# Block attention of a prompt: dividing by the row sum on the output tile, with sample pieces two rounds earlier

## The chip, the cores and the metric

The kernel runs on one core of a Trainium2 chip. Its engines are TensorE (PE, matrix products, with PEld for its weight loads), VectorE (DVE), ScalarE (ACT), GpSimd (POOL) and SyncE (SP, which here issues the loads). The metric is the device time of one execution in microseconds (us); less is better. The kernel before takes 1871.77 us, the median of three runs (1870.25 to 1883.65).

## The reference: what is computed

The reference is one inference step of a two-layer decoder trunk, in float32, for a prompt of 512 tokens and for 8 samples of 8 new tokens each, with 1024 cached tokens behind every sample. Layer 0 runs a state space mixer (S5) beside block-sparse attention (8 heads of 64); layer 1 runs HGRN2 beside stick-breaking attention; each layer ends with an output projection, a ConvFFN and a gated embedding. The change touches the attention of layer 0 for the prompt alone. Cut to that:

```
logits = jnp.einsum('bhqd,bhqnkd->bhqnk', q_c, kg) * scale        # scale = 64 ** -0.5
mask = val_c[..., None] & (kpos <= pos_c[None, None, :, None, None])
logits = jnp.where(mask, logits, NEG)
w = jax.nn.softmax(logits.reshape(bsz, nh, qc, nsel * MOBA_BLOCK), axis=-1).reshape(logits.shape)
return jnp.einsum('bhqnk,bhqnkd->bhqd', w, vg)
```

With 512 prompt tokens there are two blocks of 256, so that for the prompt every block in the past is selected, and the result is plain causal attention. For the samples there are four cached blocks of which three are kept, and the new tokens; this part is unchanged and is done in what the text calls the samples' pieces.

## The kernel before, in words

The work of layer 0 before the attention leaves queries and keys in `zqk` (head dimension on the partitions, two heads to a column c) and values in `vt` (tokens on the partitions). The order on every engine is written out by hand; the engines meet through counting semaphores. A fence (all three compute engines wait for each other) stands ahead of the attention stage and behind it.

The stage works through 32 units `UNITS`: head pair c (4), query tile i of 128 tokens (4), and the two heads hh of the pair. A unit has i+1 key tiles, so 128 to 512 keys. Its steps are: PE writes the scores (L1492) into one of two PSUM banks; DVE adds the causal mask on the last 128 columns (L1575), takes the row maximum (L1576) and scales it (L1579); ACT takes the exponential into SBUF and sums each row (L1544); DVE takes the reciprocal of the sum (L1585) and multiplies the probabilities by it (L1586); PE transposes them, 128 columns at a time (L1520), into two other banks; ACT copies them to SBUF (L1554); PE multiplies with the values (L1504), two heads side by side on 64 output rows each, with the values as weights, into bank 4, in which the output of a head pair collects; ACT copies that to `y` once for four query tiles (L1532). Each engine has a loop over rounds u: in round u PE does the scores of u+1, the transpositions of u-1 and, in odd rounds, the outputs of the pair of units u-3 and u-2; DVE does the maximum of u and the normalisation of u-1; ACT the exponential of u and the copy of u-1.

At the end of a round `between` runs pieces of the samples' attention. There are four sample pairs, each a generator on PE, ACT and DVE whose pieces are due at round 8 i + d, with d from the table `DUE_A`. PE's six pieces of a pair are: key products of the first and second sample (L1383 and, behind the second, L1390 for the new tokens' keys), transpositions of the weights (L1397, L1398), value products of the first and second sample (L1408), turn of the output (L1416). DVE's five: scores of the new tokens and block sums (L1617, L1619); block maxima (L1621, L1622); choice of blocks (L1624 to L1631); scaling of the output (L1634, L1635, L1461); copies to `y` (L1468). ACT's three: two pieces of exponentials (L1595, L1599), and the copy of the transposed weights (L1425, L1426). The cached keys and values come by DMA, 256 KB a page of 128 tokens, in an order that SP waits out (`sp_stream`); a buffer is filled again when PE has used it (`k_used`, `v_used`).

For the last pair, DVE's fourth piece begins with `dve_out_first` (L372), the low part of the output projection's first weights and of half of `y`; it waits for ACT's part of the same, `act_out_first` (L369), which ACT does in its round 32. The projection itself is L606, behind the fence.

## Time and profile before

| | us |
|---|---|
| median of three runs | 1871.77 (1870.25 to 1883.65) |
| the profiled execution, its own time | 1887.05 |
| its span, first to last instruction | 1885.3 |
| attention stage of layer 0, in the span | 211.9 to 328.7, 116.8 long |
| PE busy over the span | 1787.7 (95%) |
| DVE busy | 1134.8 (60%) |
| ACT busy | 734.1 (39%) |

Busy time counts instructions of an engine; matrix products overlap each other and their weight loads, so a busy PE is not a PE at its peak. PEclk is the clock that PE was granted, as a share of 2.4 GHz. The chain of waits follows the work that ended last back in time; a piece of it has a start, a length, and the engine and line. f32 products show as two instructions each.

### The profile page before, as it was taken

The page shows a single profiled execution, that of the slowest core. Times are in us where ns is not written, and L with a number is a line of the kernel's source. Part 1 is how long each engine was busy: PE and PEld are TensorE (multiplying, and loading weights), DVE is VectorE, ACT ScalarE, POOL GpSimd, SP SyncE. Part 2 cuts the span into 40 slices and gives each one's busy share as a digit, 9 for nine tenths or more (in the row PEclk, how much of TensorE's full clock was granted, in tenths as well). Part 3 has the DMA queues.
Part 4 walks back from the last instruction along what each step waited for, and adds up shares of the span by engine and source line. Part 5 has one row for each costly group of instructions (what it writes and reads, how often), then busy time and mean ns, then how long its engine had stood idle before and what let it go on. Part 6 is the DMA issues. An engine that isn't in the chain of part 4 may idle for free.

```text
span 1885.3 us, 34376 instructions
## 1 busy us (share of the span) xinstructions
PE 1787.7 (95%) x13464; PEld 1622.6 (86%) x13464; DVE 1134.8 (60%) x2371; ACT 734.1 (39%) x1321; POOL 36.0 (2%) x65
## 2 busy tenths in 40 slices
PE   6899798999999999999999998888999999999997
PEld 5789455999999999989799985445999999999997
DVE  7975356568777762256525855666468777762264
ACT  5222335553333342256323323656553333342253
POOL 1400000000000000000000000000000000000000
PEclk9999788999999999999999996989999999999999
DMA  4124577313222232132121142863313222132111
GB/s 182 66 28 163 204 267 288 112 43 100 79 88 78 64 132 81 47 118 79 51 95 57 57 150 96 313 225 122 111 35 98 81 79 88 54 136 79 71 64 51
DMA packets 77953, 204.18 MB, mean 108 GB/s; under 512 B 12530, under 2 KB 14882, under 8 KB 77314
## 3 DMA queue, kind: packets, MB, share of 16 engines
q1 hardware_dynamic: 75762, 190.36, 29.8%
q0 software_dynamic: 2064, 12.06, 1.7%
q8 instruction: 88, 1.44, 0.3%
q14 instruction: 39, 0.32, 0.1%
HBM read 190.81 MB, written 10.40 MB: 107 GB/s over the span
## 4 chain that ended last, share of the span: by engine, by line
PE 86%; DVE 8%; ACT 2%; issue 2%; DMA 2%; SPq 1%; DVEq 0%; ACTq 0%; POOLq 0%
PE psum L412 29%; PE psum L1946 15%; PE psum L606 13%; PE psum L2346 7%; PE psum L2303 3%; PE psum L420 3%; PE psum L1408 2%; PE psum L1383 2%; PE psum L865 2%; PE psum L2496 1%; PE psum L526 1%; PE psum L540 1%; PE psum L1492 1%; PE psum L1520 1%; PE psum L2559 1%
## 5 line engine op out<-in xcount | busy, mean ns | idle before, releaser
L412 PE MATMUL psum<-sb_a_sb_r,sb_ring_r 128*128 128x288 f32 x1408 | 297.6, 296 | 0.0
L412 PE MATMUL psum<-sb_a_sb_r,sb_arena_r 128*128 128x288 f32 x1344 | 276.5, 296 | 0.0
L412 PE MATMUL psum<-sb_y_sb_r,sb_ring_r 128*128 128x288 f32 x960 | 263.3, 299 | 0.6 <-DVE sb_ring_r L372 0.6
L412 PEld LDWEIGHTS psum<-sb_a_sb_r,sb_ring_r 128*128 128x128 f32 x1408 | 231.3, 188 | 0.3
L372 DVE TENSOR_TENSOR sb_ring_r<-sb_ring,sb_ring_r 128x1024 fp32r<-128x1024 f32 (+1 forms) x90 | 116.2, 1295 | 177.7 <-ACT sb_ring_r L369 176.7
L412 PEld LDWEIGHTS psum<-sb_a_sb_r,sb_arena_r 128*128 128x128 f32 x1344 | 217.0, 188 | 0.0
L412 PE MATMUL psum<-sb_y_sb_r,sb_arena_r 128*128 128x288 f32 x704 | 207.2, 294 | 6.3 <-DVE sb_a_sb_r L372 6.2
L369 ACT ACTIVATE sb_ring_r<-sb_ring 128x1024 fp32r<-128x1024 f32 (+1 forms) x90 | 99.9, 1114 | 289.2 <-PE psum L412 172.3
L412 PEld LDWEIGHTS psum<-sb_y_sb_r,sb_ring_r 128*128 128x128 f32 x960 | 175.5, 190 | 1.5 <-DVE sb_ring_r L372 1.0
L369 ACT ACTIVATE sb_arena_r<-sb_ring 128x1024 fp32r<-128x1024 f32 x90 | 92.9, 1055 | 171.6 <-PE psum L412 149.5
L606 PE MATMUL psum<-sb_arena_r 128*128 128x288 f32 x960 | 156.9, 297 | 1.0 <-DVE sb_arena_r L372 0.9
L1946 PE MATMUL psum<-sb_arena_r,sb_ring_r 128*128 128x288 f32 x1056 | 142.9, 295 | 0.5 <-issue 0.5
L1946 PE MATMUL psum<-sb_arena_r,sb_y_sb_r 128*128 128x288 f32 x1056 | 142.4, 295 | 0.1
L1946 PEld LDWEIGHTS psum<-sb_arena_r,sb_ring_r 128*128 128x128 f32 x1056 | 141.0, 188 | 0.9 <-issue 0.9
L412 PEld LDWEIGHTS psum<-sb_y_sb_r,sb_arena_r 128*128 128x128 f32 x704 | 134.6, 191 | 8.2 <-DVE sb_ring_r L372 6.3
L1946 PEld LDWEIGHTS psum<-sb_arena_r,sb_y_sb_r 128*128 128x128 f32 x1056 | 140.5, 188 | 0.5 <-issue 0.5
L606 PEld LDWEIGHTS psum<-sb_arena_r 128*128 128x128 f32 x960 | 138.6, 188 | 2.4 <-DVE sb_arena_r L372 1.4
L372 DVE TENSOR_TENSOR sb_arena_r<-sb_ring,sb_arena_r 128x1024 fp32r<-128x1024 f32 x74 | 89.3, 1223 | 68.0 <-ACT sb_arena_r L369 67.4
L565 DVE SCALAR_TENSOR_TENSOR sb_a_sb<-sb_a_sb,sb_vec,sb_rstd 128x288 f32<-128x288 f32 x96 | 48.3, 514 | 81.5 <-ACT sb_rstd L513 81.5
L2346 PE MATMUL psum<-sb_a_sb_r,sb_ring_r 128*128 128x288 f32 x448 | 92.0, 297 | 0.0
L372 DVE TENSOR_TENSOR sb_y_sb_r<-sb_ring,sb_y_sb_r 128x1408 fp32r<-128x1408 f32 x16 | 26.0, 1625 | 90.1 <-ACT sb_y_sb_r L369 90.1
L606 PE MATMUL psum<-sb_y_sb_r,sb_arena_r 128*128 128x288 f32 x256 | 75.2, 294 | 0.0
(406 smaller groups left out, 3176.3 us busy)
## 6 DMA issues: line engine op xcount, KB each, us to landing
sb_ring<-w SPq DMA_DIRECT2D x166, 512.0 KB, 3.5
sb_ring<-wd SPq DMA_DIRECT2D x32, 704.0 KB, 4.2
sb_arena<-sb_v SPq DMA_DIRECT2D x64, 256.0 KB, 5.3
sb_arena<-moba_v SPq DMA_DIRECT2D x56, 256.0 KB, 5.3
sb_ring<-moba_k SPq DMA_DIRECT2D x32, 256.0 KB, 5.6
sb_a_sb<-moba_k SPq DMA_DIRECT2D x32, 256.0 KB, 7.5
sb_ring<-sb_k SPq DMA_DIRECT2D x32, 256.0 KB, 6.0
sb_a_sb<-sb_k SPq DMA_DIRECT2D x32, 256.0 KB, 6.5
```

The costliest lines, as they stand in the source:

```text
L369: e.eng.activation(fr(dst), src, ACT.Copy).then_inc(ready, 1)
L372: e.eng.tensor_tensor(fr(dst), src, fr(high).bitcast(F32), ALU.subtract).then_inc(ready, 1)
L412: ins = e.eng.matmul(out[:, half, :], fr(w[p][:, k, :]), fr(x[q][:, k, cols]), start=(first and k == 0 and i == 0), stop=(last and k == kb ...
L420: ins = e.eng.matmul(out[:, half, :], w[:, k, :], rhs[:, k, half * HALF:(half + 1) * HALF], start=(first and k == 0), stop=(last and k == ...
L565: e.eng.scalar_tensor_tensor(a[:, k, c], a[:, k, c], vcol(layer, gain, k), rstd[:, c], ALU.mult, ALU.mult)\
L606: ins = e.eng.matmul(out, fr(w[p][:, k, :]), fr(x[q][:, k, COLS[half]]), start=(k == 0 and i == 0), stop=(k == KD - 1 and i == 2))
L865: last = e.eng.matmul(psum[0:n, 2 * t.s, :], fr(x[:, k, i * P:i * P + n]), fr(w[:, :, k, :]), start=(k == 0 and j == 0), stop=(k == KD - 1 ...
L1383: last = pe.matmul(psum[32 * c:32 * c + 32, 5 + half, :], qz[:, c, i, s, :], keys[:, 4 * half:4 * half + 4, c, :], start=(s == 0), stop=(s ...
L1408: last = pe.matmul(s_out[32 * c:32 * c + 32, s * P:(s + 1) * P], wt[0:rows, g, 32 * c:32 * c + 32], v[0:rows, c * P:(c + 1) * P], start=(g ...
L1946: last = e.eng.matmul(pair(t.s)[:, half, :], fr(dsplit[part][i // 2][:, k, :]), fr(x[:, COLS[half]]), start=(j == 0 and i == 0), stop=(j = ...
L2303: last = e.eng.matmul(psum[0:n, 2 * t.s, :], fr(x[:, k, i * P:i * P + n]), fr(w[:, :, k, :]), start=(k == 0 and z == 0), stop=(k == KD - 1 ...
L2346: last = e.eng.matmul(pair(t.s)[:, half, :], fr(pair_c(m)[p][:, k, :]), fr((a, y)[q][:, k, COLS[half]]), start=(k == 0 and i == 0), stop=( ...
```

## The change

The probabilities are no longer multiplied by the reciprocal row sum. They go to the transposition as the exponential left them, and the division is done on the unit pair's output. For that the output products swap their operands: the transposed probabilities (128 keys x 128 queries) are the weights and 64 value columns are streamed, so the output of two heads stands as 128 queries x 128 columns in bank 3 or 4; DVE takes two reciprocals at once (L1596) and multiplies each head's 64 columns from PSUM into SBUF (L1600), PE turns the tile (L1520 of the new kernel) and ACT copies it to `y` (L1543), once a pair instead of once in four. The transposed probabilities are written back into the unit's own score bank, and three banks take turns. A unit's transpositions now stand ahead of the scores of the unit two later. Row maxima, sums and reciprocals have rings of 4 and 8 columns. The samples' pieces are due two rounds earlier on PE, ACT and DVE, and the loops end at round 37 instead of 33 or 32.

```diff
--- before.py
+++ after.py
@@ -1302,7 +1302,7 @@
             for x in range(u, 8 * NPAIR + 16) if u == last else [u]:
                 for i, p in enumerate(pieces):
                     for d in units:
-                        if apart * i + d == x:
+                        if max(apart * i + d, 0) == x:
                             next(p, None)
 
         kv_in = [sem(f"kv_in{i}") for i in range(4)]
@@ -1472,13 +1472,18 @@
 
         pb = [cut(unit_at + i * 512, 512) for i in range(2)]
         ptb = [cut(unit_at + (2 + i) * 512, 512).rearrange("p (j n) -> p j n", j=4) for i in range(4)]
-        stat = small[:, 8:64]
-
-        sco_ready, nmx_ready, prob_ready, pn_ready, ptr_ready, pt_ready, o_unit, o_copied = (
-            sem(x) for x in ("sco_ready", "nmx_ready", "prob_ready", "pn_ready", "ptr_ready", "pt_ready", "o_unit", "o_copied"))
-        UNITS = [(2 * c + hh, i) for c in range(4) for i in range(4) for hh in range(2)]
-
-        DUE_A = {"pe": (8, (1, 2, 6, 7, 8, 9)), "act": (8, (5, 5, 6)), "dve": (8, (3, 4, 5, 9, 9))}
+        onb = [cut(unit_at + 6 * 512 + i * P, P) for i in range(2)]
+        assert unit_at + 6 * 512 + 2 * P <= 27952
+        most, nmost, total, share = (small[:, 8 + 8 * i:16 + 8 * i] for i in range(4))
+
+        sco_ready, nmx_ready, prob_ready, ptr_ready, pt_ready, o_unit, o_normed, o_turned, o_copied = (
+            sem(x) for x in ("sco_ready", "nmx_ready", "prob_ready", "ptr_ready", "pt_ready", "o_unit", "o_normed",
+                             "o_turned", "o_copied"))
+        PAIRS = [(c, i) for c in range(4) for i in range(4)]
+        UNITS = [(2 * c + hh, i) for c, i in PAIRS for hh in range(2)]
+
+        DUE_A = {"pe": (8, (-1, 0, 4, 5, 6, 7)), "act": (8, (3, 3, 4)), "dve": (8, (1, 2, 3, 7, 7))}
+        LAST_A = len(UNITS) + 5
 
         def pe_moba_prompt(e):
             pe = e.eng
@@ -1487,78 +1492,84 @@
             def scores(u):
                 hh, i = UNITS[u]
                 r0, c, n = 64 * (hh % 2), hh // 2, P * (i + 1)
-                if u >= 2:
-                    pe.wait_ge(prob_ready, u - 1)
-                pe.matmul(psum[:, u % 2, 0:n], zqk[r0:r0 + 64, c, i * P:(i + 1) * P], zqk[r0:r0 + 64, 4 + c, 0:n],
+                if u >= 3:
+                    pe.wait_ge(pt_ready, u - 2)
+                pe.matmul(psum[:, u % 3, 0:n], zqk[r0:r0 + 64, c, i * P:(i + 1) * P], zqk[r0:r0 + 64, 4 + c, 0:n],
                           start=True, stop=True).then_inc(sco_ready, 1)
 
-            def outputs(u):
-                c, i = UNITS[u][0] // 2, UNITS[u][1]
-                pe.wait_ge(pt_ready, u + 2)
-                if i == 0 and c >= 1:
-                    pe.wait_ge(o_copied, c)
-                for j in range(i + 1):
-                    for x in (u, u + 1):
-                        hh = UNITS[x][0]
-                        r0 = 64 * (hh % 2)
-                        last = pe.matmul(psum[r0:r0 + 64, 4, i * P:(i + 1) * P],
-                                         vt[:, j, hh * HD:(hh + 1) * HD], ptb[x % 4][:, j, :],
-                                         start=(j == 0), stop=(j == i))
-                        if j == i:
-                            last.then_inc(o_unit, 1)
+            def turned(u):
+                pe.wait_ge(prob_ready, u + 1)
+                for j in range(UNITS[u][1] + 1):
+                    last = pe.transpose(psum[:, u % 3, j * P:(j + 1) * P], pb[u % 2][:, j * P:(j + 1) * P], ident)
+                last.then_inc(ptr_ready, 1)
+
+            def outputs(p):
+                c, i = PAIRS[p]
+                pe.wait_ge(pt_ready, 2 * p + 2)
+                if p >= 2:
+                    pe.wait_ge(o_copied, p - 1)
+                for hh in range(2):
+                    at = (2 * c + hh) * HD
+                    for j in range(i + 1):
+                        last = pe.matmul(psum[:, 3 + p % 2, HD * hh:HD * hh + HD], ptb[(2 * p + hh) % 4][:, j, :],
+                                         vt[:, j, at:at + HD], start=(j == 0), stop=(j == i))
+                    last.then_inc(o_unit, 1)
+
+            def output_turned(p):
+                pe.wait_ge(o_normed, p + 1)
+                pe.transpose(psum[:, 3 + p % 2, P:2 * P], onb[p % 2], ident).then_inc(o_turned, 1)
 
             scores(0)
-            for u in range(len(UNITS) + 2):
-                if u + 1 < len(UNITS):
-                    scores(u + 1)
+            scores(1)
+            for u in range(LAST_A + 1):
                 if 1 <= u <= len(UNITS):
-                    hh, i = UNITS[u - 1]
-                    pe.wait_ge(pn_ready, u)
-                    if u >= 3:
-                        pe.wait_ge(pt_ready, u - 2)
-                    for j in range(i + 1):
-                        last = pe.transpose(psum[:, 2 + (u - 1) % 2, j * P:(j + 1) * P],
-                                            pb[(u - 1) % 2][:, j * P:(j + 1) * P], ident)
-                    last.then_inc(ptr_ready, 1)
-                if u >= 3 and u % 2 == 1:
-                    outputs(u - 3)
-                between(samples, u, len(UNITS) + 1, DUE_A["pe"])
+                    turned(u - 1)
+                    if u + 1 < len(UNITS):
+                        scores(u + 1)
+                if u % 2 == 1:
+                    p = u // 2
+                    if 1 <= p <= len(PAIRS):
+                        outputs(p - 1)
+                    if 2 <= p <= len(PAIRS) + 1:
+                        output_turned(p - 2)
+                between(samples, u, LAST_A, DUE_A["pe"])
 
         def act_moba_prompt(e):
             act = e.eng
 
-            def copy_out(c):
-                act.wait_ge(o_unit, 8 * (c + 1))
-                act.activation(y[:, 4 + c, 0:TP], psum[:, 4, :], ACT.Copy).then_inc(o_copied, 1)
+            def copy_out(p):
+                c, i = PAIRS[p]
+                act.wait_ge(o_turned, p + 1)
+                act.activation(y[:, 4 + c, i * P:(i + 1) * P], psum[:, 3 + p % 2, P:2 * P], ACT.Copy).then_inc(o_copied, 1)
 
             act.wait_ge(stored, 16 * 5)
             act.preload_act_table_set("natural_log_exp_and_others")
             samples = [act_moba_sample(e, i) for i in range(NPAIR)]
-            for u in range(len(UNITS) + 1):
+            for u in range(LAST_A + 1):
                 if u < len(UNITS):
-                    hh, i = UNITS[u]
-                    n = P * (i + 1)
+                    n = P * (UNITS[u][1] + 1)
                     act.wait_ge(nmx_ready, u + 1)
                     if u >= 2:
                         act.wait_ge(ptr_ready, u - 1)
-                    act.activation(pb[u % 2][:, 0:n], psum[:, u % 2, 0:n], ACT.Exp, scale=ATT_SCALE,
-                                   bias=stat[:, 2 + u % 2:3 + u % 2], accum_out=stat[:, 4 + u % 2:5 + u % 2])\
+                    if u >= 8:
+                        act.wait_ge(o_normed, (u - 8) // 2 + 1)
+                    act.activation(pb[u % 2][:, 0:n], psum[:, u % 3, 0:n], ACT.Exp, scale=ATT_SCALE,
+                                   bias=nmost[:, u % 4:u % 4 + 1], accum_out=total[:, u % 8:u % 8 + 1])\
                        .then_inc(prob_ready, 1)
                 if u == len(UNITS):
                     act_out_first(e, 0, sco_ready)
-                if u >= 1:
-                    hh, i = UNITS[u - 1]
+                if 1 <= u <= len(UNITS):
+                    i = UNITS[u - 1][1]
                     act.wait_ge(ptr_ready, u)
                     if u >= 5:
                         act.wait_ge(o_unit, u - 4)
-                    act.activation(ptb[(u - 1) % 4][:, 0:i + 1, :], psum[:, 2 + (u - 1) % 2, 0:P * (i + 1)]
+                    act.activation(ptb[(u - 1) % 4][:, 0:i + 1, :], psum[:, (u - 1) % 3, 0:P * (i + 1)]
                                    .rearrange("p (j n) -> p j n", j=i + 1), ACT.Copy).then_inc(pt_ready, 1)
-                if u >= 10 and (u - 10) % 8 == 0:
-                    copy_out((u - 10) // 8)
+                if u >= 6 and u % 2 == 0:
+                    copy_out((u - 6) // 2)
                 if u == len(UNITS):
                     act_slab(e, out_pairs[1], 1)
-                    copy_out(3)
-                between(samples, u, len(UNITS), DUE_A["act"])
+                between(samples, u, LAST_A, DUE_A["act"])
 
         def dve_moba_prompt(e):
             v, do = e.eng, e.st.do
@@ -1566,26 +1577,30 @@
             dve_queries(e)
             samples = [dve_moba_sample(e, i) for i in range(NPAIR)]
             causal = lcon[:, LCON[0]["causal"]:LCON[0]["causal"] + P]
-            for u in range(len(UNITS) + 1):
+            for u in range(LAST_A + 1):
                 if u < len(UNITS):
-                    hh, i = UNITS[u]
+                    i = UNITS[u][1]
                     n = P * (i + 1)
                     v.wait_ge(sco_ready, u + 1)
-                    own = psum[:, u % 2, i * P:n]
+                    own = psum[:, u % 3, i * P:n]
                     do(v.tensor_tensor(own, own, causal, ALU.add))
-                    do(v.tensor_reduce(stat[:, u % 2:u % 2 + 1], psum[:, u % 2, 0:n], AXX, ALU.max))
-                    if u >= 2:
-                        v.wait_ge(prob_ready, u - 1)
-                    v.tensor_scalar(stat[:, 2 + u % 2:3 + u % 2], stat[:, u % 2:u % 2 + 1], -ATT_SCALE, None, ALU.mult)\
+                    do(v.tensor_reduce(most[:, u % 4:u % 4 + 1], psum[:, u % 3, 0:n], AXX, ALU.max))
+                    if u >= 4:
+                        v.wait_ge(prob_ready, u - 3)
+                    v.tensor_scalar(nmost[:, u % 4:u % 4 + 1], most[:, u % 4:u % 4 + 1], -ATT_SCALE, None, ALU.mult)\
                      .then_inc(nmx_ready, 1)
-                if u >= 1:
-                    w = u - 1
-                    n = P * (UNITS[w][1] + 1)
-                    v.wait_ge(prob_ready, w + 1)
-                    do(v.reciprocal(stat[:, 6 + w % 2:7 + w % 2], stat[:, 4 + w % 2:5 + w % 2]))
-                    v.tensor_scalar(pb[w % 2][:, 0:n], pb[w % 2][:, 0:n], stat[:, 6 + w % 2:7 + w % 2], None, ALU.mult)\
-                     .then_inc(pn_ready, 1)
-                between(samples, u, len(UNITS), DUE_A["dve"])
+                if u >= 4 and u % 2 == 0 and (u - 4) // 2 < len(PAIRS):
+                    p = (u - 4) // 2
+                    at = 2 * p % 8
+                    v.wait_ge(o_unit, 2 * p + 2)
+                    do(v.reciprocal(share[:, at:at + 2], total[:, at:at + 2]))
+                    if p >= 2:
+                        v.wait_ge(o_turned, p - 1)
+                    for hh in range(2):
+                        last = v.tensor_scalar(onb[p % 2][:, HD * hh:HD * hh + HD], psum[:, 3 + p % 2, HD * hh:HD * hh + HD],
+                                               share[:, at + hh:at + hh + 1], None, ALU.mult)
+                    last.then_inc(o_normed, 1)
+                between(samples, u, LAST_A, DUE_A["dve"])
 
 
         def act_moba_sample(e, i):
```

PE's order over rounds 2 to 7 of the first pair in the kernel before (L1492 scores, L1520 transpositions, L1504 outputs, L1397 and L1398 the samples' weights; repeats of a unit's rows are left out at the ends):

```order
L1492 MATMUL psum<-sb_arena 128x512
L1520 MATMUL psum<-sb_con,sb_arena 128x128 x3
L1504 MATMUL psum<-sb_arena 64x128 x4
L1492 MATMUL psum<-sb_arena 128x512
L1520 MATMUL psum<-sb_con,sb_arena 128x128 x3
L1397 MATMUL psum<-sb_con,sb_arena 128x128 x8
L1398 MATMUL psum<-sb_con,sb_arena 64x128
L1492 MATMUL psum<-sb_arena 128x128
```

The same place in the changed kernel (L1497 scores, L1503 transpositions, L1514 outputs, L1520 turn of an output):

```order
L1503 MATMUL psum<-sb_con,sb_arena 128x128 x2
L1497 MATMUL psum<-sb_arena 128x384
L1397 MATMUL psum<-sb_con,sb_arena 128x128 x8
L1398 MATMUL psum<-sb_con,sb_arena 64x128
L1503 MATMUL psum<-sb_con,sb_arena 128x128 x3
L1497 MATMUL psum<-sb_arena 128x512
L1514 MATMUL psum<-sb_arena 128x64 x4
L1520 MATMUL psum<-sb_con,sb_arena 128x128
```

Both score products of 512 keys stood ahead of the samples' weight transpositions, and now stand behind them; a product of 384 keys is the last in front.

DVE's order at the end of the stage before, from the last normalisations (L1585, L1586) through the last pair's fourth and fifth pieces:

```order
L1585 RECIPROCAL sb_small<-sb_small 128x1
L1586 TENSOR_SCALAR sb_arena<-sb_arena,sb_small 128x512
L1634 TENSOR_REDUCE sb_arena<-sb_arena 128x1
L1635 RECIPROCAL sb_arena<-sb_arena 128x1
L372 TENSOR_TENSOR sb_ring_r<-sb_ring,sb_ring_r 128x1024
L372 TENSOR_TENSOR sb_y_sb_r<-sb_y_sb,sb_arena_r 128x288 x4
L1461 TENSOR_SCALAR sb_arena<-psum,sb_arena 128x256
L1468 COPY sb_y_sb<-psum 64x4x8 x4
```

And now (L1590 is the scale of the last unit's maximum, L1596 and L1600 the division of a pair's output):

```order
L1590 TENSOR_SCALAR sb_small<-sb_small 128x1
L1649 TENSOR_REDUCE sb_arena<-sb_arena 128x1
L1650 RECIPROCAL sb_arena<-sb_arena 128x1
L372 TENSOR_TENSOR sb_ring_r<-sb_ring,sb_ring_r 128x1024
L372 TENSOR_TENSOR sb_y_sb_r<-sb_y_sb,sb_arena_r 128x288 x4
L1461 TENSOR_SCALAR sb_arena<-psum,sb_arena 128x256
L1468 COPY sb_y_sb<-psum 64x4x8 x4
L1596 RECIPROCAL sb_small<-sb_small 128x2
L1600 TENSOR_SCALAR sb_arena<-psum,sb_small 128x64 x2
L1596 RECIPROCAL sb_small<-sb_small 128x2
```

The division of the last two pairs' outputs stands behind the split and the samples' last pieces, where nothing of the prompt stood before.

## Rows read from the trace of the kernel before

**Rows 1.** The page, first part: busy us, share, instructions.
```profile
PE 1787.7 (95%) x13464; PEld 1622.6 (86%) x13464; DVE 1134.8 (60%) x2371; ACT 734.1 (39%) x1321; POOL 36.0 (2%) x65
```
**Rows 2.** Windows: stretch, length, busy us of PE, PEld, DVE, ACT, POOL, clock, DMA.
```profile
211.90:328.70 116.80, 105.23 (x1116) 59.48 (x1117) 71.70 (x248) 51.87 (x156) 0.00 (x0) 0.81 0.73 260
254.00:255.00 1.00, 0.30 (x1) 0.00 (x0) 0.93 (x5) 0.42 (x1) 0.00 (x0) 1.00 1.03 381
256.00:265.00 9.00, 8.57 (x28) 4.45 (x28) 6.43 (x25) 4.81 (x18) 0.00 (x0) 0.50 1.05 389
265.00:266.00 1.00, 1.00 (x6) 0.65 (x6) 0.41 (x2) 1.00 (x3) 0.00 (x0) 0.77 0.76 281
```
**Rows 3.** Chain of waits through the stage: start us, us, engine and line.
```profile
223.76 0.27 PE psum L1390 x16
...
251.66 0.27 PE psum L1390 x16
...
256.43 0.31 DVE psum L1575
...
258.09 0.90 PE psum L1520 x3
...
262.88 1.71 PE psum L1397 x8
...
266.92 2.24 PE psum L1408 x72
...
277.41 1.85 PE psum L1383 x16
...
306.65 0.27 PE psum L1390 x16
```
**Rows 4.** Chain of waits, single steps at the full clock: scores, transpositions, outputs; last L2496.
```profile
241.55 0.42 PE psum L1492 x2
241.97 0.59 PE psum L1520 x4
...
244.79 0.63 PE psum L1492 x2
245.42 0.26 PE psum L1520
...
273.28 1.02 PE psum L1504 x16
...
1037.66 3.52 PE psum L2496 x32
```
**Rows 5.** Groups of instructions by shape, DVE, 205 to 345 us: busy us, mean ns | idle.
```profile
L1576 DVE TENSOR_REDUCE sb_small<-psum 128x1 f32<-128x256 f32 x8 | 3.4, 424 | 0.3
L1585 DVE RECIPROCAL sb_small<-sb_small 128x1 f32<-128x1 f32 x32 | 4.9, 154 | 3.9 <-ACT sb_arena L1544 3.9
L1586 DVE TENSOR_SCALAR sb_arena<-sb_arena,sb_small 128x512 f32<-128x512 f32 x8 | 3.9, 487 | 0.3
L1586 DVE TENSOR_SCALAR sb_arena<-sb_arena,sb_small 128x128 f32<-128x128 f32 x8 | 2.3, 288 | 0.3
L1617 DVE SCALAR_TENSOR_TENSOR sb_arena<-psum,sb_lcon 128x64 f32<-128x64 f32 x4 | 0.9, 225 | 3.8 <-PE psum L1390 3.8
```
**Rows 6.** Timeline: start us, us; DVE's piece three begins, ACT's last exponential of the sample ends.
```profile
257.95 0.15 DVE L1624 TENSOR_REDUCE sb_arena<-sb_arena 128x1 f32<-128x4 f32 x1
261.69 0.21 ACT L1599 ACTIVATION_READ_ACCUMULATOR sb_arena<-sb_arena 128x1 f32 x1
```
**Rows 7.** Timeline at the start of the stage: DVE's copies of the samples' queries.
```profile
213.23 0.99 DVE L1436 COPY sb_arena<-sb_arena 64x128 f32<-64x128 f32 x4
```
**Rows 8.** Timeline at the end of the stage: the split ahead of the output projection.
```profile
321.92 1.06 ACT L369 ACTIVATE sb_ring_r<-sb_ring 128x1024 fp32r<-128x1024 f32 x1
323.08 1.22 DVE L372 TENSOR_TENSOR sb_ring_r<-sb_ring,sb_ring_r 128x1024 fp32r<-128x1024 f32 x1 [0.55 <-ACT sb_ring_r L369]
324.23 1.56 DVE L372 TENSOR_TENSOR sb_y_sb_r<-sb_y_sb,sb_arena_r 128x288 fp32r<-128x288 f32 x4
```

## The prediction

> **What bounds the kernel now.** I read the busy slices of the page first, then the windows of the block-attention stage, then its chain of waits, and last the timeline of single rounds. The page [rows 1] shows TensorE (PE) busy for 95% of the span, so that a stage with less is worth a look. The stage of the change, from 211.9 to 328.7 us [rows 2], is one: 116.8 us, 6% of the span, PE busy 105.2 with a mean granted clock of 0.81, VectorE (DVE) 71.7. Nothing outside it is edited, so all that follows is a sum over these 116.8 us.
>
> Within it the samples' pieces come four times, every 8 rounds. The piece that ends a pair's key products, L1390, starts at 223.76 for the first, 251.66 for the second and 306.65 for the fourth [rows 3]: a period of 27.6 us. Take the one that begins at 251.93, where that piece ends. Up to 258.09 the chain runs through DVE; from there to the next L1390 it stays on PE [rows 3]. In the DVE part PE runs out of work (busy 0.30 us between 254 and 255), and its clock falls from 1.00, which is 2.4 GHz, to 0.50, 1.2 GHz, through 256 to 265; in 265 to 266 it is back on 1.00 for about half (0.77) [rows 2], some 7 us after PE's work began again at 258.09 [rows 3]. So there are three costs in a period: PE's own work, a stretch that DVE sets, and low clock behind it.
>
> **PE's work in a round, then and now.** At the full clock the chain gives 0.42 us for a score product of 128 keys and 0.63 for 256, so 0.21 more for each 128: 0.84 and 1.05 for 384 and 512. One transposition costs 0.26, four 0.59, so 0.11 more for each [rows 4]. These pieces keep their cost; only where they stand changes. The output products change form. Before, sixteen L1504 instructions (64-column weights) take 1.02 us, 64 ns each [rows 4]. After, the probabilities are the 128x128 weights and 64 value columns stream. The nearest row is L2496, f32, 128x128 weights and 64 columns: 32 in 3.52 us, **110 ns each** [rows 4]. The stage has 160 of them (80 products, two instructions each), so 17.6 us against 10.2, plus 16 new transpositions of the output at 0.26 or less (the chain's single one), 4.2 us at most. I take 110 ns because that row has the same weights, type and columns; the lower bound is the old 64 ns.
> The Trainium skill (TensorE: Matmul & The Clock Gate, LDWEIGHTS) puts a weight load at columns / 1.2, an estimate of 107 ns for 128 columns, and L2496 agrees. The same page's table in Back-to-back issue gap has about 60 cycles for up to 64 moving columns, 25 ns; by it the 160 would cost 4 us, a saving of 6 us instead of a loss of 7. The trace decides for the first.
>
> Rounds u mod 8 of the new order, at the full clock (transpositions of u-1, scores of u+1, outputs, output turn, sample piece): round 1 is .26+.63+1.76+.26 = 2.9; round 2 .9; round 3 1.9; round 4 .37+.84 = 1.2 and then the samples' nine weight transpositions, 1.14; round 5 .48+1.05+.88+.26 and V0 2.24 = 4.9; round 6 .48+1.05+2.24 = 3.8; round 7 .59+.42+1.32+.26+.37+1.85 = 4.8; round 0 .59+.42+2.12 = 3.1. V is a sample's value products, 2.24, and a sample's key products are 1.85, with 0.27 for L1390 after the second [rows 3]; .37 is the two turns of the sample's output. The sum is **24.7**, against 21.9 for the old pieces by the same rows.
>
> **DVE's share.** Removed are 32 reciprocals at 154 ns and 32 normalisations, 288 ns (128 columns) to 487 ns (512) [rows 5]: 4.9 + 12.4 = 17.3 us. Added are 16 times a reciprocal and two 128x64 operations from PSUM; the nearest row is L1617, 225 ns [rows 5], so 0.55 with its waits, 8.8 us. DVE does 8.5 us less. The score part of a round is the mask (the chain's 0.31), the maximum (0.42 for 256 keys), a small scale like the reciprocal's 0.15, and gaps: 0.95 for 256 keys, and 0.13 more for 384 [rows 3, 5].
>
> **What the two rounds do.** DVE's first three sample pieces move from rounds 3, 4, 5 to 1, 2, 3, ScalarE's (ACT) exponentials to round 3, PE's nine transpositions from 6 to 4. The way from the end of L1390 to these: DVE's pieces one and two lay between 251.93 and 256.43 together with one score part of 384 keys (1.08), a reciprocal of which 0.08 shows and a normalisation of 256 columns (0.35), so they take 4.50-1.51 = 2.99 [rows 3]. In the new rounds 1 to 3 two score parts of 256 keys (.95 each) and one output share (.55) lie among them. Piece three and ACT's exponentials run from 257.95 to 261.90, 3.95 [rows 6], and .1 goes for issue: 2.99+.95+.55+.95+3.95+.1 = **9.5**. PE has only 2.9+.9+1.9+1.2 = 6.9 us to do there, so it waits 2.6. Before, the chain reaches L1397 at 262.88, 10.9 after the same point, but both products of 512 keys had run by then; now they stand behind. Behind the wait stand 1.14+4.9+3.8+4.8+3.1 = 17.8 us of PE. So 9.5+17.8 = 27.3 with the clock never low.
> The gap before the transpositions will cost clock as the old one did. If it returns 7 us after the restart, those 7 us hold the nine transpositions, 1.92 instead of 1.14 (L1397's eight took 1.71 at the low clock), three at .90 for .48 (the chain's at 258.09), and the 512-key scores and the outputs at double, 2.0 and 1.76 for 1.05 and .88 [rows 3, 4]: 3.1 us and with the output's turn 3.2. The bounds are 0 and 3.2; I take 2.5, nearer to the end that before shows. Period: **29.8**, against 27.6.
>
> **Start.** Both key pieces now stand before the first transposition and need the queries, ready at 214.22 [rows 7]. At the low clock the first takes twice 1.85, 3.7; the second ends with L1390 at 220.0 to 222.0, as the clock comes back. I take 221.0; before 224.0 [rows 3]. Gain 3.0 (2 to 4). The key and value transfers run at 381 to 389 GB/s through 254 to 265 and fall to 281 in 265 to 266 [rows 2]; the keys are used after the value products that start at 266.92 and the next ones [rows 3], so they land with a few us to spare. The moves keep their distances and the period grows, so I cost the transfers at nothing; if they were late, that would add. SP's own queue keeps its order. POOL does nothing here.
>
> **End.** After the last L1390 (before: 306.92) two more rounds are left than before. PE ends the last value piece at 9.5+1.1+4.9+3.8+2.5 = 21.8, its next transposition at 22.4. DVE's last sample piece, now in round 31, begins with the split for the output projection, and that waits for ACT: a copy (about .6), the slab 1.06; then DVE 1.22 and 1.56, and a scale near L1586's .49 [rows 5, 8] = 27.4. Before, these ran beside PE's last value products. Now PE's turn of the sample output waits for them, and behind it the last unit: .37+.59, copy .6, outputs 1.76, share .55, turn .26, copy .3, fence .25, with gaps 32.4. Before it is 328.7-306.9 = 21.8 [rows 2, 3].
>
> **Sum.** 221.0 + (29.8-.55, no share in the first) + 2x29.8 + 32.4 = 342.2, against 328.7: +13.5. The wait of about 3.4 us in the last round may leave the clock low for the last outputs and the projection's start: 0 to 5.7 us (2.2 in the tail, 3.5 in 7 us of projection); I take 2. **+15.5 us, 0.8%.** The sum is against the profiled execution, 1887.05 us, which lies 15 us above the median; its span's stage is the only one I have, so I put the difference on the median: 1871.8+15.5 = **1887.3**. The low ends together (clock always full, 220.0) give 331.3, +2.6; the high ends (222.0, 3.2 a period, 5.7 at the end) give +23.
>
> **Rivals.** A measurement of this kernel tells about 1%, 18.7 us, from no change.
> *Same way, clock low longer*: over 1% slower, +18.7 to +23, if the clock returns late in each period and the projection starts low. For it: the low stretch of 256 to 265 outlasted the restart by 7 us, and idle time now comes later and longer; against: both stretches must bite, in every period. 0.24.
> *The clock stays full*: +2.6 to +8. For it: PE now works through rounds 1 to 3, with no gap before round 4. Against: PE's 0.7 idle us in 254 to 255 were followed by the fall [rows 2]. 0.12.
> *PE-paced, faster than before*: one mechanism, in rounds 3 and 4: the sample softmax on DVE and ACT is ready by 6.9 instead of 9.5 after L1390, because the share and the maxima fit in DVE's holes. Then nothing waits: 9.1 + 3x24.7 + a tail of 23.5 (16.7 of rounds and 6.8 for the last units) = 106.7, 10 us less: 1861.7. It decides at 2.6 us off a chain whose every row is measured; 0.09. Beyond that no mechanism reaches 1% (98 us for the stage is below PE's 4x24.7): 0.02.
> *The change moves nothing that matters* (no time on the path differs): 0.03. The forecast itself, +8 to +18.7: 0.50.
> So faster 0.02, same 0.50+0.12+0.09+0.03 = 0.74, slower 0.24. The range 1868 to 1896 takes the forecast, the full clock and the late clock up to +24, and leaves out the PE-paced case and the far ends, under 0.2.
>
> **What the profile after would show.** Right: L1514 at about 110 ns each; L1390 starts near 220.7 and then 29 to 30.5 apart; PE idle 2 us or more before L1397, released by ACT's exponentials; idle before the last L1416, released by DVE's L1461; stage over 125 us. Wrong: L1514 near 64 ns or less, a period at or under 27, no idle at L1397, or a fence before 329.

## The result, and the profile after

The changed kernel takes a median of 1904.0 us (1898.23 to 1907.05, 4 runs) against 1872.74 us (1870.25 to 1883.65, 4 runs) for the kernel before. The ratio of the two kernels over all their runs is **1.0146, interval 1.012 to 1.0173** (the two medians by themselves would give 1.0167): 22 to 32 us slower. The forecast was 1887.3 us with a range up to 1896, so the direction of the sum was right and its size too small by about 12 us of the 27. The profiled execution takes 1907.05 us, its span is 1905.3 us.

The page after, first part (busy us, share of the span, instructions); it answers to [rows 1]:

```profile
PE 1802.1 (95%) x13480; PEld 1640.4 (86%) x13480; DVE 1128.6 (59%) x2355; ACT 735.1 (39%) x1333; POOL 38.4 (2%) x65
```

DVE has 16 instructions less, as the diff says, and 6.2 us less, where the prediction had 8.5; PE has 16 more, and 14.4 us more. The same 95% share hides both. Windows of the stage after, with the columns of [rows 2]: first the whole stage, from the first score product to the first product of the output projection (L606), then stretches with a low clock:

```profile
208.25:346.57 138.32, 119.63 (x1133) 76.76 (x1133) 65.74 (x232) 52.45 (x167) 0.00 (x0) 0.78 0.62 219
257.00:268.00 11.00, 11.00 (x96) 7.93 (x96) 1.79 (x6) 3.58 (x11) 0.00 (x0) 0.50 0.24 87
289.00:292.00 3.00, 2.54 (x12) 2.39 (x12) 0.62 (x2) 1.73 (x8) 0.00 (x0) 0.50 0.86 315
317.00:329.00 12.00, 10.91 (x95) 7.95 (x95) 3.01 (x11) 4.93 (x17) 0.00 (x0) 0.50 0.40 149
337.00:346.00 9.00, 5.79 (x24) 4.92 (x24) 3.69 (x15) 1.99 (x4) 0.00 (x0) 0.50 0.19 59
```

The stage takes 138.3 us instead of 116.8 and its mean clock is 0.78 instead of 0.81. From 257 to 268 PE is busy for every one of 11 us and the clock is still 0.50: this is not waiting, it is the same work at half the speed. Windows of 1 us (stretch, length, PE busy, clock, DMA) date the changes of the clock, estimated from a window's mean clock; two of them:

```profile
254.00:255.00 1.00, 0.75 (x2) 0.89 1.04 381
268.00:269.00 1.00, 1.00 (x4) 0.79 0.13 20
```

By such windows the clock falls at 220.6, 254.8, 288.9 and 316.2 and is back at 234.3, 268.4, 292.3 and 329.9; it falls once more at 336.7 and comes back in the projection. Each fall comes before PE's restart at L1397 (225.16, 256.74, 289.45, 318.08), the first one 4.5 us before it, while PE works: PE had stood idle for 1.50 us before 219.34. So idle time in the rounds ahead of L1397 stands before a fall too, and not only the wait in front of it.

The chain of waits through the stage after (start us, us, engine and line) says which work that is:

```profile
215.85 0.28 PE psum L1390 x16
...
246.70 0.22 PE psum L1390 x16
...
247.81 1.94 PE psum L1514 x16
...
256.74 1.97 PE psum L1397 x8
...
259.56 2.00 PE psum L1497 x2
261.56 1.90 PE psum L1514 x8
...
263.67 4.15 PE psum L1408 x72
...
279.42 0.22 PE psum L1390 x16
...
289.45 1.97 PE psum L1397 x8
...
293.37 1.03 PE psum L1514 x8
...
294.52 2.24 PE psum L1408 x72
...
308.05 0.22 PE psum L1390 x16
...
318.08 1.97 PE psum L1397 x8
...
325.02 4.15 PE psum L1408 x72
...
338.71 0.69 PE psum L1416 x2
...
341.20 3.65 PE psum L1514 x16
...
346.57 33.59 PE psum L606 x240
```

L1390 still marks the end of a pair's key products. Its starts are 30.85, 32.72 and 28.63 apart, against 27.6 in [rows 3] (three periods, called the first, second and third). Behind L1397 in the second period, the 512-key scores (L1497) take 2.00, eight output products (L1514) 1.90 and the value products (L1408) 4.15; at the full clock, in the third period or in [rows 3], the last two take 1.03 and 2.24. The timeline after shows the two waits that the prediction asked for (the first with two rows, weight load and product):

```profile
256.73 0.50 PEld L1397 LDWEIGHTS psum<-sb_con,sb_arena 128*128 128x128 f32 x3 [2.60 <-ACT sb_arena L1614]
256.74 0.69 PE L1397 MATMUL psum<-sb_con,sb_arena 128*128 128x128 f32 x2 [1.98 <-ACT sb_arena L1614]
...
338.71 0.69 PE L1416 MATMUL psum<-sb_con,sb_arena 128*128 128x128 f32 x2 [3.43 <-DVE sb_arena L1461]
```

And the new operations by shape, 205 to 350 us (busy us, mean ns | idle before them); the L1600 and L1596 rows answer to L1586 and L1585 of [rows 5]:

```profile
L1514 PE MATMUL psum<-sb_arena 128*128 128x64 f32 x160 | 25.8, 319 | 0.9 <-ACT sb_y_sb L1543 0.9
...
L1600 DVE TENSOR_SCALAR sb_arena<-psum,sb_small 128x64 f32<-128x64 f32 x32 | 7.6, 280 | 0.6
L1520 PE MATMUL psum<-sb_con,sb_arena 128*128 128x128 f32 x16 | 5.2, 327 | 0.6 <-DVE sb_arena L1600 0.6
...
L1596 DVE RECIPROCAL sb_small<-sb_small 128x2 f32<-128x2 f32 x16 | 2.6, 160 | 7.0 <-PE psum L1514 7.0
```

A mean of 319 ns for L1514 counts products that overlap one another. What each adds to the chain at the full clock is 121 ns (1.94 us for 16 instructions), and 129 ns where there are only eight (1.03 us).

### The profile page after: what moved, and what is told of

Same layout as the page of the kernel before. It is cut to its first block, busy times and chain, and to the rows that moved or that the text cites. A ratio compares the mean times of both kernels' runs of the same rounds, so it can differ in the third digit from the quotient of the medians.

```text
span 1905.3 us, 34397 instructions
## 1 busy us (share of the span) xinstructions
PE 1802.1 (95%) x13480; PEld 1640.4 (86%) x13480; DVE 1128.6 (59%) x2355; ACT 735.1 (39%) x1333; POOL 38.4 (2%) x65
## 4 chain that ended last, share of the span: by engine, by line
PE 85%; DVE 8%; ACT 3%; issue 2%; DMA 2%; SPq 1%; DVEq 0%; ACTq 0%; POOLq 0%
PE psum L412 28%; PE psum L1961 15%; PE psum L606 13%; PE psum L2361 7%; PE psum L2318 3%; PE psum L420 2%; PE psum L1408 2%; PE psum L1383 2%; PE psum L865 1%; PE psum L2511 1%; PE psum L526 1%; PE psum L1514 1%; PE psum L540 1%; PE psum L1497 1%; PE psum L2574 1%
## 5 line engine op out<-in xcount | busy, mean ns | idle before, releaser
L606 PE MATMUL psum<-sb_arena_r 128*128 128x288 f32 x960 | 156.9, 297 | 1.0 <-DVE sb_arena_r L372 0.9
L606 PEld LDWEIGHTS psum<-sb_arena_r 128*128 128x128 f32 x960 | 138.6, 188 | 2.4 <-DVE sb_arena_r L372 1.4
L606 PE MATMUL psum<-sb_y_sb_r,sb_arena_r 128*128 128x288 f32 x256 | 75.2, 294 | 0.0
```

What stands on the lines that cost most here:

```text
L606: ins = e.eng.matmul(out, fr(w[p][:, k, :]), fr(x[q][:, k, COLS[half]]), start=(k == 0 and i == 0), stop=(k == KD - 1 and i == 2))
```

## The experiments

**Theory 1**: the pieces moved two rounds ahead open PE's gap before the samples' weight transpositions (L1397), and the clock that falls in it stays low over the work behind. **The rival**, Theory 2 in the expectations: the new arithmetic (products with the probabilities as weights, division and turn of the output) is what costs, whatever the order. What each says in numbers stands with each run.

A stage has three parts: from its first scores to the end of the first L1390, three periods, and the rest to the first L606. From the chain of each run's one profiled execution, us:

| kernel | start | three periods | end | stage | ratio to before [interval] |
|---|---|---|---|---|---|
| before | 12.1 | 82.9 | 21.8 | 116.8 | 1 |
| predicted | 9.1 | 88.9 | 32.4 | 130.3 | |
| after | 7.9 | 92.1 | 38.3 | 138.3 | 1.0146 [1.012, 1.0173] |
| e8, after again | 8.1 | 94.6 | 37.2 | 139.9 | 1.0144 [1.0128, 1.0159] |
| e1, after, old order | 12.2 | 87.8 | 22.4 | 122.4 | 1.0032 [1.0014, 1.005] |
| e2, before, new order | 8.1 | 91.5 | 35.4 | 135.0 | 1.0122 [1.0086, 1.0159] |
| e9, before, one round | 9.1 | 84.1 | 27.2 | 120.3 | 1.0033 [1.002, 1.0046] |
| e3, after, old products | 8.5 | 81.8 | 31.5 | 121.8 | 1.0088 [1.0058, 1.0117] |
| e6, after, split later | 8.0 | 94.6 | 32.5 | 135.2 | 1.0106 [1.0081, 1.0132] |
| e4, after, 2 dead products | 8.5 | 88.1 | 32.9 | 129.6 | 1.0126 [1.0097, 1.0155] |
| e10, after, 3 dead products | 8.0 | 82.5 | 32.8 | 123.3 | 1.0057 [1.0036, 1.0079] |
| e12, e1 with e4's | 11.3 | 80.8 | 22.7 | 114.7 | 1.0019 [1.0002, 1.0035] |

**e1_due_back.** The changed kernel with the old table of rounds.

```diff
-        DUE_A = {"pe": (8, (-1, 0, 4, 5, 6, 7)), "act": (8, (3, 3, 4)), "dve": (8, (1, 2, 3, 7, 7))}
+        DUE_A = {"pe": (8, (1, 2, 6, 7, 8, 9)), "act": (8, (5, 5, 6)), "dve": (8, (3, 4, 5, 9, 9))}
```

> The changed kernel with the samples' pieces due where they were before (table with 1, 2, 6, 7, 8, 9 for PE, 5, 5, 6 for ACT, 3, 4, 5, 9, 9 for DVE); the division on the output, the score banks and the loops' ends stay as changed. Theory 1 (the two rounds cost most: the samples' softmax has too little PE work in front of it, both 512-key products run behind it at the low clock, and the last split has no cover): a period near 28.3 us, no wait before the last L1416, the stage 120 to 125 us against 138.3, so 14 to 18 us less than the changed kernel, 1878 to 1886. Theory 2 (the swapped output products at 110 ns, and not the rounds, cost most): hardly under the changed kernel, 1895 or more, ratio to before at least 1.011.

1883.72 us against 1876.88, ratio 1.0032. Its stage, with the columns of [rows 2]:

```profile
210.58:332.99 122.41, 107.71 (x1133) 68.87 (x1133) 65.58 (x232) 51.75 (x167) 0.00 (x0) 0.89 0.70 248
```

It issues the same instructions as the changed kernel (x1133 on PE) and PE is busy for 12 us less. Most of the loss goes with the order; the new arithmetic alone costs 3 to 9 us.

**e2_due_only.** The kernel before, with the new table alone.

```diff
-                        if apart * i + d == x:
+                        if max(apart * i + d, 0) == x:
...
-        DUE_A = {"pe": (8, (1, 2, 6, 7, 8, 9)), "act": (8, (5, 5, 6)), "dve": (8, (3, 4, 5, 9, 9))}
+        DUE_A = {"pe": (8, (-1, 0, 4, 5, 6, 7)), "act": (8, (3, 3, 4)), "dve": (8, (1, 2, 3, 7, 7))}
```

> The kernel before with only the new due table (samples' pieces two rounds earlier on all engines), nothing else of the change. Theory 1: most of the loss is here too: the period grows by 2 to 4 us and the tail has the wait for the split, 8 to 18 us above before, 1881 to 1891. Theory 2: within 4 us of before, or faster by the 3 to 4 us that the start gains.

1901.54 us against 1876.88, ratio 1.0122. Its stage:

```profile
208.10:343.08 134.98, 115.39 (x1116) 64.67 (x1117) 71.58 (x248) 52.15 (x155) 0.00 (x0) 0.75 0.63 225
```

The old arithmetic in the new order already has the loss: 18.2 us on the stage, at a clock of 0.75. With e1's 5.6 us the two halves make 23.8, where the two traces of the whole change show 21.5 and 23.1; they add up to within the 1.6 us by which the two traces differ.

**e9_one_round.** The kernel before, its pieces one round ahead instead of two.

```diff
-        DUE_A = {"pe": (8, (1, 2, 6, 7, 8, 9)), "act": (8, (5, 5, 6)), "dve": (8, (3, 4, 5, 9, 9))}
+        DUE_A = {"pe": (8, (0, 1, 5, 6, 7, 8)), "act": (8, (4, 4, 5)), "dve": (8, (2, 3, 4, 8, 8))}
```

> The kernel before with the samples' pieces one round earlier instead of two, nothing else. Two rounds cost 23 us (ratio 1.0122). If the cause is what stands in front of the samples' weight transpositions and of the last split (one 512-key product of the two is back in front, one value piece is back beside the split), one round costs between a third and two thirds of that, ratio 1.004 to 1.008. If the loss comes only with the second round (the start or the ring of buffers), the ratio is under 1.003.

1880.56 us against 1874.65, ratio 1.0033, just under what was expected. One round costs about a quarter of what two cost in e2. The periods hardly grow (84.1 for 82.9), and in its chain L1397 stands right behind PE's own transpositions and outputs (L1504) with no wait between, so it is the second round that opens the wait at L1397; the end grows by 5.4 us a round at first and by 8.2 with the second.

**e3_old_form.** The changed kernel with the value columns as weights again.

```diff
-                for hh in range(2):
-                    at = (2 * c + hh) * HD
-                    for j in range(i + 1):
-                        last = pe.matmul(psum[:, 3 + p % 2, HD * hh:HD * hh + HD], ptb[(2 * p + hh) % 4][:, j, :],
-                                         vt[:, j, at:at + HD], start=(j == 0), stop=(j == i))
-                    last.then_inc(o_unit, 1)
+                for j in range(i + 1):
+                    for hh in range(2):
+                        at = (2 * c + hh) * HD
+                        last = pe.matmul(psum[HD * hh:HD * hh + HD, 3 + p % 2, 0:P], vt[:, j, at:at + HD],
+                                         ptb[(2 * p + hh) % 4][:, j, :], start=(j == 0), stop=(j == i))
+                        if j == i:
+                            last.then_inc(o_unit, 1)
```

> The changed kernel with its output products in the old form (64 value columns as weights, the 128 probabilities streamed, two heads side by side), written to the same banks; everything behind them runs as changed, so the division and the turn work on a tile that stands the wrong way, and the output of the prompt's attention is not the reference's. Theory 1: L1514 back to about 64 ns at the full clock, 7.4 us less at full clock and up to 12 with what ran at the low one: 1892 to 1898. Theory 2: most of the 27 us goes, 1885 or less.

1893.99 us against 1876.88, ratio 1.0088, about 10 us under the changed kernel and inside what Theory 1 gave. The form itself is worth 7.4 us in the sum (160 times 110 less 64 ns). In its profiled execution the clock was back 2.7 to 2.9 us after every L1397, so its stage shows a larger gain (121.8 for 138.3) than the 10 us of the timed runs.

**e5_no_norm.** The kernel before without reciprocal and normalisation.

```diff
-                    pe.wait_ge(pn_ready, u)
+                    pe.wait_ge(prob_ready, u)
...
-                    v.wait_ge(prob_ready, w + 1)
-                    do(v.reciprocal(stat[:, 6 + w % 2:7 + w % 2], stat[:, 4 + w % 2:5 + w % 2]))
-                    v.tensor_scalar(pb[w % 2][:, 0:n], pb[w % 2][:, 0:n], stat[:, 6 + w % 2:7 + w % 2], None, ALU.mult)\
-                     .then_inc(pn_ready, 1)
```

> The kernel before without the division by the row sum (L1585 and L1586 left out, PE's transpositions wait for the exponential instead; the prompt's attention output is then not divided, so not the reference's). It is what the change takes from DVE, 17 us of work, with nothing added in its place and no rounds moved. If DVE's division is what holds the period: 0.4 to 1 us less in each of the rounds 3 to 6, 1.5 to 3 us a period, 6 to 12 us less than before in all. If PE's own work and the clock hold it: within 4 us of before.

1877.3 us against 1875.05, ratio 1.0006 [0.9992, 1.0021]: the second of the two cases, within 4 us of before. Its trace has 64 DVE instructions and 15.2 us of DVE's busy time less in the stage (17.3 by [rows 5]). The whole relief that the change aims at is worth nothing that can be told, even when nothing is added for it: at most 1.5 us by the interval.

**e6_split_later.** The changed kernel; DVE's split for the output projection moves from before its last sample piece to round 33.

```diff
-            if i == NPAIR - 1:
+            if i == NPAIR - 1 and n >= NPAIR:
                 dve_out_first(e)
...
+                if u == len(UNITS) + 1:
+                    dve_out_first(e)
                 between(samples, u, LAST_A, DUE_A["dve"])
```

> The changed kernel with DVE's split for the output projection (L372, 2.8 us) taken out of the last pair's fourth piece and done in round 33, behind the division of the last pair but one, so that the samples' output and the last unit no longer wait for it. If the wait for the split is part of the loss: the wait of 3.4 us before the last L1416 goes and some of the low clock of the tail with it, 4 to 8 us less than the changed kernel. If the last unit's own chain sets the end: 0 to 3 us.

1895.83 us against 1875.05, ratio 1.0106, some 7 us under the changed kernel, though the intervals just overlap. Its periods are those of e8, its end is 32.5 instead of 37.2 us. So the split in front of the last L1416 is about 5 us of the end in these two traces.

**e8_after_again.** The changed kernel unedited, to see what differs between two executions.

> The changed kernel again, unedited, on the same chip and beside the same runs of before as the other three: a ratio of 1.012 to 1.017, and a second trace, which shows how far stages without an edit differ between two runs (HGRN took 43 to 54 us in the traces so far).

1902.11 us against 1875.05, ratio 1.0144. Its chain:

```profile
217.77 0.28 PE psum L1390 x16
...
248.71 0.22 PE psum L1390 x16
...
279.92 0.22 PE psum L1390 x16
...
312.45 0.22 PE psum L1390 x16
...
349.88 2.26 PE psum L606 x8
```

Here the third period is the long one (32.53), in the first trace it was the second (32.72) and the third was short (28.63). One order of instructions, one kernel: how long the clock stays low is not fixed by them. It is back 9.3, 8.4, 11.3 and 9.5 us after PE's restart at L1397 (by windows of 1 us).

**e4_fill.** The changed kernel with two dead products of 512 columns, into a bank whose contents have been used, just ahead of PE's wait for the sample's softmax.

```diff
+            if layer == 0:
+                for _ in range(2):
+                    pe.matmul(psum[:, 7, :], ident, con[:, 0:512], start=True, stop=True)
             pe.wait_ge(sw_ready, n + 1)
```

> The changed kernel with two dead f32 products (identity as weights, 512 columns, 1.7 us at the full clock, into the bank of the samples' new scores, whose contents have been used) ahead of PE's wait for the samples' softmax, four times in the stage. If the low clock behind that wait is the larger part of what the sum missed, the clock stays at 1.00 or comes back earlier, V0 (L1408) takes 2.24 everywhere and the time falls by 6 to 14 us. If the low clock begins earlier than the filler or the filler only delays the work behind it, the time stays or rises by up to 6 us.

1900.09 us against 1876.88, ratio 1.0126. Its interval overlaps that of the changed kernel: inconclusive. In its trace the dead products themselves ran at the low clock in three of four places, wholly or in part, so the clock had fallen before them, in the rounds ahead where PE also waits for DVE and ACT.

**e10_fill3.** As e4, and a third dead product at the start of round 4.

```diff
+            if layer == 0:
+                for _ in range(2):
+                    pe.matmul(psum[:, 7, :], ident, con[:, 0:512], start=True, stop=True)
...
+                if u % 8 == 4 and u < len(UNITS):
+                    pe.matmul(psum[:, 7, :], ident, con[:, 0:512], start=True, stop=True)
```

> The changed kernel with three dead products of 512 columns in round 4 of every eight (one ahead of the round's transpositions, two ahead of the samples' weight transpositions, 2.6 us at the full clock), one more than before, to cover nearly all of PE's 3 idle us there. If the clock falls because of that idle time, it stays at 1.00 up to the transpositions in most periods, L1397 takes about 1.1 instead of 1.97, periods are 28 to 29 us and the ratio 1.008 to 1.011. If low clock is not what lengthens the periods, the ratio stays at 1.0145 or rises by 0.001 to 0.003, as the dead products delay the work.

1884.99 us against 1874.65, **ratio 1.0057**, its interval clear of the changed kernel's: some 16 us are gained by adding work. Its chain, then a window over nearly three periods:

```profile
245.67 0.22 PE psum L1390 x16
...
255.71 1.09 PE psum L1400 x8
...
272.97 0.22 PE psum L1390 x16
...
300.27 0.22 PE psum L1390 x16
```

```profile
246.00:322.00 76.00, 75.46 (x809) 46.56 (x808) 42.43 (x151) 34.89 (x115) 0.00 (x0) 1.00 0.80 289
```

The clock is 1.00 from 246 to 322, the sample's transpositions (L1400 here) take 1.09 instead of 1.97, and the period is 27.3 us: the number that the prediction's sum had for a clock that is never low. The way to the transpositions is no shorter (245.89 to 255.71, 9.8 us); DVE and ACT still set most of it. PE filled its wait and got its clock. What is left of the loss in this trace is the end, 11.0 us, less 4.1 at the start, and 2.3 us in the projection (34.3 for 32.0). The dead products do not reach the last wait, the one for the split; there the clock is low again, and L1514 x16 (L1517 here) takes 3.65 us as in the changed kernel:

```profile
324.00:338.00 14.00, 10.56 (x43) 9.63 (x44) 7.52 (x21) 6.91 (x16) 0.55 (x1) 0.54 0.24 69
```

**e7_before_fill.** The kernel before with one dead product of 512 columns in rounds 4 and 5 of 8, where its own gap lies.

```diff
-                    pe.wait_ge(pn_ready, u)
                     if u >= 3:
                         pe.wait_ge(pt_ready, u - 2)
+                    if u % 8 in (4, 5):
+                        pe.matmul(psum[:, 2 + (u - 1) % 2, :], ident, con[:, 0:512], start=True, stop=True)
+                    pe.wait_ge(pn_ready, u)
```

> The kernel before with one dead f32 product of 512 columns (0.85 us at the full clock, into the transposition bank that the next transpositions overwrite) in rounds 4 and 5 of every eight, ahead of PE's wait for the division. If low clock behind DVE's stretch costs the 3.6 us a period that its rows suggest: the clock stays at 1.00 in most periods and the time falls by 4 to 12 us. If the fall is set by more than these two gaps: no change, or up to 4 us slower.

1873.17 us against 1875.05, ratio 0.9993 [0.9974, 1.0011]: expected was a gain of 4 to 12 us, and none is proven. The profiled stage takes 111.3 us at a clock of 0.94:

```profile
213.20:324.50 111.30, 100.62 (x1132) 54.91 (x1133) 71.70 (x248) 51.55 (x156) 0.00 (x0) 0.94 0.77 273
```

That is 5.5 us less than the one trace of the kernel before, and the timed runs don't follow it. A single trace of this stage is good to some microseconds only.

**e11_fill_start.** As e7, with two more dead products in round 0.

```diff
+                if u == 0:
+                    for _ in range(2):
+                        pe.matmul(psum[:, 2, :], ident, con[:, 0:512], start=True, stop=True)
```

> The kernel before with the dead products in rounds 4 and 5 and two more in round 0, behind the second score product, while PE waits for the first maxima (bank 2, not used yet). If the clock comes back earlier at the start of the stage, the first key products take less than 3.6 us and 2 to 4 us more are gained: ratio 0.996 to 0.999. If not, as with the fillers alone, 0.999.

1875.04 us against 1874.65, ratio 1.0002 [0.9987, 1.0016]. No gain, although its trace shows the sign that was asked for: the first key products take 1.85 us instead of 3.57, and the stage 112.8.

**e12_back_fill.** The changed kernel with e1's edit (old table) and e4's (two dead products): the new arithmetic with the low clock taken off it.

> The changed kernel with the due table of before and the two dead products (1.7 us at the full clock) ahead of PE's wait for the samples' softmax: the rounds' place and the low clock are both taken out, so what is left against before is the new form of the division alone. With the table back alone two of four periods had the low clock (stage 122.4 us, ratio 1.0032). If the dead products keep it full, periods of 27 us or less and a stage of 118 to 121 us: ratio 0.999 to 1.002, and the new division is then worth about nothing, PE's 110 ns products against DVE's 8.5 us. If the new division has a gain that the low clock hid, the ratio is 0.997 or less.

1880.36 us against 1875.94, ratio 1.0019 [1.0002, 1.0035]. In its trace the clock is full from 219 to 325 and the stage is 2.1 us shorter than before's, but the projection is 2.3 us longer (34.3). Even so the new arithmetic gains nothing in the timed runs. No version is faster than the kernel before by more than its interval.

## Why the prediction was wrong

**What held.** L1514 takes 121 ns on the chain (110 taken, 64 the lower bound); L2496 in [rows 4] was the right neighbour. The Trainium skill (TensorE: Matmul & The Clock Gate, Back-to-back issue gap) has about 60 cycles, 25 ns, for up to 64 moving columns, for a product by itself with no weight load in it. This trace, where every product has fresh weights, does not come near it. The way from the end of L1390 to L1397 is 246.92 to 256.74, 9.8 us (9.5), and between 9.0 and 9.8 in all four places; the 0.3 over is DVE's wait for L1514 ahead of its first share (0.32 at 249.78), which the sum did not have. PE is idle before L1397 and before the last L1416, released by the instructions named, for 2.0 us (1.0 in the first place; 2.6 foretold, which the weight load's wait reaches) and 3.4 us. The start gains 4.2 us (3.0). No transfer, and nothing on SP or POOL, stands in the chain. With the clock held up in the periods (e10), a period takes 27.3 us, as in the sum, and the stretch from L1397 to the end of the next L1390 takes 17.5 for 17.8. In the last stretch DVE's L1461 ends 24.9 us after L1390, which is the forecast's 27.4 without its 2.5 for the clock. So the structure of the sum stands. That e10's whole end, 32.8, comes near the forecast's 32.4 is luck: e10 has none of the 2.5 us that the forecast put behind the fourth L1397, and 2.9 us of low clock in its last unit, where the forecast's 32.4 has none. The sign "29 to 30.5 apart" did not come: all three periods lie outside it.

**The step that failed** is the cost of the low clock behind the gap: "If it returns 7 us after the restart", with "The bounds are 0 and 3.2; I take 2.5". The 7 us came from the one low stretch that the prediction looks at. The other three of the kernel before say the same: the clock is back 7.9, 7.4, 7.1 and 7.0 us after the four restarts at L1520 (230.26, 258.09, 285.69, 313.08). The windows of the third and fourth, columns as above:

```profile
292.00:293.00 1.00, 1.00 (x4) 0.62 1.04 383
...
320.00:321.00 1.00, 1.00 (x15) 0.97 0.92 341
```

The new order did not keep it. After, the clock comes back 9 us (234.3), 12 us (268.4), 3 us (292.3) and 12 us (329.9) after PE's restart at L1397. Past 7 us it catches the value product, which costs 4.15 for 2.24. From L1397 to the end of the next L1390 the chain takes 21.8, 22.9 and 18.8 us (in e8 21.9, 21.4 and 22.7) where the sum has 17.8: **4.0, 5.1 and 1.0 us** more (in e8 4.1, 3.6, 4.9), where the forecast put 2.5, so the upper bound of 3.2 was no bound. Over the three periods that is 3.3 us more than the forecast (5.8 in e8).

The end is short by 5.9 us through the same term, twice. Its "9.5+1.1+4.9+3.8+2.5 = 21.8" has 2.5 for the low clock behind the fourth L1397, and that was too small again: PE's last value product ends 25.0 us after L1390, and DVE's L1461 30.4 after it, not 27.4. Against e10's 24.9 the low clock costs 5.5 us there, so 3.0 of the miss. And the last unit runs wholly in the low clock of the wait before L1416: L1514 x16 takes 3.65 instead of 1.94, and from L1461 to the fence it is 7.9 us, not 5.0. That is the other 2.9, nearly all of it PE's rows at the low clock. The 2 us taken for this stood outside the 32.4, for the last outputs and the projection together, where 2.9 and 1.6 were measured (the projection's 240 products take 33.6, before 32.0). With the start 1.2 better, the stage is 8.0 over its 130.3.

**The rival** "same way, clock low longer" is what happened, but its +18.7 to +23 was worked out with the same bounds, so it ended at +23 and the range at +24.

**The rest of the miss.** The stage differs by 21.5 us, or 23.1 in e8, the projection by 1.6; the ratio says 22 to 32. These agree, and what lies above 25 us can't be placed. The traces' spans differ by only 20.0 us, because the stage begins 3.6 us earlier after. I put the sum onto the median while the execution of before was 15 us above it. Part of that excess lies far from the change: one stage of layer 1, the HGRN2 mixer with the same instructions in all, takes 53.1 us in that trace and 45.3 in e8 (first before, then e8):

```profile
1115.90:1169.00 53.10, 44.73 (x194) 35.67 (x194) 23.62 (x54) 9.53 (x11) 1.11 (x2) 0.69 0.39 150
```

```profile
1138.00:1183.30 45.30, 36.68 (x194) 27.50 (x194) 23.67 (x54) 9.67 (x12) 1.11 (x2) 0.83 0.46 174
```

The clock makes it, 0.69 and 0.83. No instruction of that stage was changed, so this speaks for the median as the base; no run shows it.

**Where the 27 us are from**, by the runs: the order costs some 16 to 30 us by e2's interval and the arithmetic 3 to 9 (e1). Seen the other way, about 16 of the 27 are low clock, since e10 takes them away. The rest is in the main two rounds more behind the last L1390 (11.0 us at the end, 4.1 back at the start), of which 2.9 us at the end, and 2.3 in the projection, are low clock too that e10 leaves.

**Open**: what decides, from one period to the next, when the clock comes back. The instructions ahead of it are the same in the second and third period. That the dead products work through PE's activity and not through a changed order of arrivals is argued from the window at 1.00, not shown by a run that fills the gap with anything else.

## What to carry to other kernels

A gap on PE has two prices: the wait, and half speed for the work behind it. Put no upper bound on the second from the old order: four low stretches of the kernel before agreed on 7 to 8 us, and the new order gave 3 to 12. Price every row that could stand behind the gap, the costly value product above all, and count every gap, those of the ramp at the end too. Before relieving an engine that shows 60% busy, run the kernel with the work simply left out: here that gained nothing (e5). Moving pieces ahead of time put their wait where PE had nothing left to do.

## What the runs showed of the hardware

- The clock can stay at 0.50 while PE is busy without a break: 11.00 of 11 us from 257 to 268. It came back 3 to 12 us after the restart, in one kernel. The Trainium skill (TensorE: Matmul & The Clock Gate, What's actually happening) says that the number of slow products differs from run to run of the same kernel; the traces agree, and the two traces of the changed kernel show it between periods of one run too.
- Three dead f32 products of 512 columns per 8 rounds went with a clock of 1.00 for 76 us in the trace and gained some 16 us in the timed runs; two of them, without the one at the start of round 4, made no difference that could be told, and none was gained in the kernel before (0.9993 and 1.0002), where PE is idle for 11.6 us of the stage instead of 18.7.
- An f32 product with fresh 128x128 weights and 64 moving columns takes 110 ns (L2496, 32 in a row) to 129 ns (L1514, 8 in a row) per instruction at the full clock, the old form with 64-column weights and 128 moving 64 ns (L1504, 16 in 1.02 us).
- The transpositions (L1397, eight of 128x128 f32) take 1.09 us at the full clock and 1.97 at the low one.
